# Attention of a hybrid layer: the next pair's sums a unit sooner, a half taken ahead of exponentials, and a first weight's low part put forward

## The reference

```python
def rms_norm(x, g):
    y = xf * lax.rsqrt(jnp.mean(xf * xf, axis=-1, keepdims=True) + RMS_EPS)
    return y * g

x = x + 0.5 * swiglu_ffn(rms_norm(x, ffn1_norm_g), w_gate, w_up, w_down)
proj = rms_norm(x, mix_norm_g) @ w_in
aq = rms_norm(aq.reshape(B, S, 8, 64), attn_q_norm_g)   # 8 heads of 64
ak = rms_norm(ak.reshape(B, S, 8, 64), attn_k_norm_g)
# each chunk of 64 queries sees its own chunk and the 8 before it
scores = einsum('bqhd,bkhd->bhqk', qc, kb) * 64 ** -0.5 + bias
p = softmax(where(key_pos >= 0, scores, -inf))
attn_out = einsum('bhqk,bkhd->bqhd', p, vb)
ro = rms_norm(hgrn2_chunkwise(...), hgrn_out_norm_g) * silu(hg)
x = x + concat([attn_out, ro]) @ w_out
x = x + 0.5 * swiglu_ffn(rms_norm(x, ffn2_norm_g), ...)
```

## Time and profile before

| | us |
|---|---|
| median of 3 runs | 1885.41 (1884.92 to 1886.67) |
| the profiled execution | 1885.16 |
| its span, first to last instruction | 1883.6 |
| TensorE busy | 1869.4 |
| VectorE busy | 1125.0 |
| ScalarE busy | 675.3 |
| GpSimd busy | 406.7 |

### The profile page before, as it was taken

The page is one execution under the profiler, slowest core; times in us unless marked ns, Lnnn a source line. Parts: engine busy times, 40 slices in busy tenths (PEclk is TensorE's granted clock), DMA queues, the critical chain, the costliest instruction groups (busy, mean ns, idle before and its releaser), DMA issues. The chain is left out here.

```text
span 1883.6 us, 24459 instructions
## 1 busy us (share of the span) xinstructions
PE 1869.4 (99%) x9171; PEld 1546.3 (82%) x9171; DVE 1125.0 (60%) x1591; ACT 675.3 (36%) x1029; POOL 406.7 (22%) x319
## 2 busy tenths in 40 slices
PE   9999999999999999999999999999999999999999
PEld 8888888888888888888888678888888888888887
DVE  6966665665546641156667874477666656655464
ACT  7422323333333533211223663353223233333332
POOL 2043422241103110002222310000434222411030
PEclk9999999999999999999999999999999999999999
DMA  5355444436866433434433510133554444368653
GB/s 182 112 196 190 146 162 168 153 138 244 318 195 197 131 122 124 138 101 140 134 132 106 162 60 1 68 112 112 196 190 146 163 167 153 138 244 306 219 192 140
DMA packets 221341, 296.52 MB, mean 157 GB/s; under 512 B 15377, under 2 KB 117913, under 8 KB 221234
## 3 DMA queue, kind: packets, MB, share of 16 engines
q1 hardware_dynamic: 206752, 262.19, 41.0%
q0 software_dynamic: 6272, 18.14, 3.0%
q10 hardware_dynamic: 8210, 14.75, 2.0%
HBM read 206.13 MB, written 92.56 MB: 159 GB/s over the span
## 5 line engine op out<-in xcount | busy, mean ns | idle before, releaser
L710 PE MATMUL ps<-hThi,whi 128*128 128x512 f32 x888 | 346.6, 390 | 0.2 <-DVE hid L1751 0.2
L712 PE MATMUL ps<-hThi,wlo 128*128 128x512 f32 x888 | 345.5, 389 | 0.0
L711 PE MATMUL ps<-hTlo,whi 128*128 128x512 f32 x888 | 345.5, 389 | 0.0
L710 PE MATMUL ps<-whi 128*128 128x512 f32 x616 | 240.0, 390 | 0.0
L712 PE MATMUL ps<-whi,wlo 128*128 128x512 f32 x616 | 239.7, 389 | 0.0
L711 PE MATMUL ps<-wlo,whi 128*128 128x512 f32 x616 | 239.6, 389 | 0.0
L710 PEld LDWEIGHTS ps<-hThi,whi 128*128 128x128 f32 x888 | 166.7, 188 | 34.9 <-issue 0.9
L712 PEld LDWEIGHTS ps<-hThi,wlo 128*128 128x128 f32 x888 | 166.7, 188 | 34.7
L711 PEld LDWEIGHTS ps<-hTlo,whi 128*128 128x128 f32 x888 | 166.7, 188 | 34.3
L710 PE MATMUL ps<-hXhi,whi 128*128 128x512 f32 x480 | 186.9, 389 | 0.8 <-issue 0.8
L712 PE MATMUL ps<-hXhi,wlo 128*128 128x512 f32 x480 | 186.8, 389 | 0.0
(11 more groups left out here) (220 smaller groups left out, 2828.7 us busy)
## 6 DMA issues: line engine op xcount, KB each, us to landing
hid_scratch<-hid SPq DMA_DIRECT2D x132, 256.0 KB, 3.3
raw<-ffn_w_gate SPq DMA_DIRECT2D x44, 512.0 KB, 3.8
raw<-ffn_w_up SPq DMA_DIRECT2D x44, 512.0 KB, 4.9
wdb<-ffn_w_down SPq DMA_DIRECT2D x44, 512.0 KB, 4.1
wd_scratch<-wdb SPq DMA_DIRECT2D x88, 256.0 KB, 4.3
raw<-hid_scratch SPq DMA_DIRECT2D x80, 256.0 KB, 2.8
rawx<-hid_scratch SPq DMA_DIRECT2D x74, 256.0 KB, 2.8
raw<-w_in SPq DMA_DIRECT2D x28, 512.0 KB, 5.4
```

The costliest lines, as they stand in the source:

```text
L710: pe.matmul(dst, ahi, bhi, start=first, stop=False, skip_group_check=onto)
L711: pe.matmul(dst, ahi, blo, start=False, stop=False, skip_group_check=onto)
L712: return pe.matmul(dst, alo, bhi, start=False, stop=last, skip_group_check=onto)
```

## The change

Three things are changed. The squares of the next pair's queries and keys are placed at units 1 and 3 of the pair in place of 1 and 4, their sums at units 2 and 4 in place of 3 and 5; the norms keep their places. ScalarE takes the first turned half ahead of the exponentials of its unit, as it already did with the last; the second and third are still taken behind them. At the start VectorE makes the first weight's low part ahead of the low part of the third tile, and TensorE runs 4 idle products in place of 6 ahead of the first product.

```diff
-SQUARE_AT, SUM_AT, NORM_AT = (1, 4), (3, 5), (6, 8)
+SQUARE_AT, SUM_AT, NORM_AT = (1, 3), (2, 4), (6, 8)
...
-            idle_products(6)
+            idle_products(4)
             products(0, 0, 1)
...
             for v in range(NV + 4):
                 if 2 <= v < NV + 2 and by_scalar(v - 2):
                     take_turned(v - 2)
-                if v < NV - NU and v % NU == TURN_QK_AT[3][2]:
-                    take_half(v // NU + 1, 3)
+                if v < NV - NU:
+                    for n in (0, 3):
+                        if TURN_QK_AT[n][2] == v % NU:
+                            take_half(v // NU + 1, n)
                 if v < NV:
...
                 if v < NV - NU:
-                    for n in range(3):
+                    for n in (1, 2):
                         if TURN_QK_AT[n][2] == v % NU:
                             take_half(v // NU + 1, n)
...
             early_norm(3, 0)
             early_lo_part(1, 0)
+            weight_lo(0, 0)
             early_lo_part(2, 0)
-            weight_lo(0, 0)
             early_lo_part(3, 0)
             weight_lo(0, 1)
```

## The result

The changed kernel takes 1888.97 us (median of 15 executions, 1888.26 to 1890.07), the kernel before 1885.40 (15, 1884.92 to 1886.67). The ratio is 1.0020, 95% interval 1.0012 to 1.0027: slower, and with 3.57 us just inside the 3.8 us (0.2%) within which, by the prediction, this kernel can't be told from no change. The profiled execution took 1888.26 us and its span is 1886.7 us, 3.1 us above the 1883.6 of before. The forecast was 1888.3.

The account below looks back on a forecast made before the run. TensorE, busy 99% of the span, was taken to bound the kernel. Terms: 4.21 us late less 1.15 sooner, net +3.1 on the profiled 1885.16, so 1888.3 us; range 1885.8 to 1890.0.

Parts of the forecast that it names:

- (a): Attention, second and third pair: first sum moved ahead of unit 3's maxima makes the next scores 0.94 us late.
- (b): Attention, second and third pair: second sum moved ahead of unit 5's maxima makes the following scores 0.52 us late.
- S7 to S8: Second pair: time between scores starting at 1061.02 and 1064.94 before the change; forecast 4.86 us in place of 3.92.
- S8 to S9: Second pair: time between scores starting at 1064.94 and 1069.37 before the change; forecast 4.95 us in place of 4.43.
- rival of late squares: Attention: ScalarE's second square ends too late, each pair losing 0.5 to 1 us again, 1889.8 to 1891.3; chance 0.14.
- rival in which the sums cost nothing: Attention: unit 3's maxima don't hold the scores, so only the take and start count, 1884.0 us; chance 0.12.
- only the first sum costs: Rival, attention: second sum and head's output are hidden, 2.98 us late, net +1.8, 1887.0 us; chance 0.10.
- (c): Attention, first pair, without head's output there: two steps between scores become 4.86 (+1.10) and 4.11 us (+0.19), 1.29 late.
- (d): Attention: sooner sums give GpSimd's powers sooner, but the normalising product keeps its place (5.58 us step unchanged), worth nothing.
- (e): Attention, each of three pairs: first turned half taken ahead of unit 7's exponentials, 0.39 us wait goes, 0.35 us gained.
- (f): Kernel start: low part swapped forward and fewer idle products, first product 0.10 us sooner; bounds 0.1 lost to 0.46 won.
- clock rival: Kernel start: granted clock falls, the first product's 12 passes at half clock cost 2.9 us more, 1891.2; chance 0.02.

Follow-up runs that it names:

- the second sum alone: Only the second square and sum moved, to units 3 and 4, against the kernel before: 1890.19 us, ratio 1.0025.
- the moved sums alone: Both squares and sums moved as in the change, start and take left as before, against the kernel before: 1890.25 us against 1885.21, ratio 1.0026.
- the last run: Start and take as changed; second and third pair: squares at units 0, 2, sums 1, 3, norms 5, 7; against the kernel before: 1882.61 us, ratio 0.9986.
- the runs by pair: Squares and sums moved in the first pair only, 1886.76 us, ratio 1.0009; in second and third only, 1888.34, ratio 1.0016; both against the kernel before.

## Why the prediction was right, and where it was not

**(a), (b), the second and third pair: right.** S7 to S8 was forecast at 4.86 us and is 4.87, S8 to S9 at 4.95 and is 4.97. The square ended in time (1067.47 + 1.04 = 1068.51, the sum at 1068.79, 0.28 us to spare where 0.1 was expected), so the rival of late squares didn't happen in the change; the second sum alone shows what it costs when it does. The rival in which the sums cost nothing fell with the moved sums alone. That only the first sum costs fell too: with both moved, 0.5 us stand at S9.

**(c), the first pair: right.** S1 to S2 is 1038.06 - 1033.19 = 4.87 us (4.86), S2 to S3 4.14 (4.11).

**(d): right.** The norm didn't move nearer to S9. In the last run, where the norms move too, S9 to S10 does get shorter.

**(e): right in place, size close.** The wait for the take went, and the maxima took over with 0.16 us, as said. S10 to S11 gained 0.35 us; S11 to the next scores lost 0.04 of it again (4.40 in place of 4.36).

**(f): about the right worth, by luck.** The first product gained 0.35 us, not 0.10. I took the end of ScalarE's high part from one execution, 14.23; in the changed kernel's it began at 13.36 in place of 13.61, and the low part followed at 14.02. That isn't the change's doing: in the profiles of the other runs this high part begins anywhere from 13.04 to 13.74, with the start changed or not. But most of the 0.35 us was given back 14 us later. Five rows of the changed kernel's timeline (PEld is TensorE's weight load, which begins a product; line 1289 keeps the first product's bank):

```profile
14.77 0.50 PE L721 MATMUL ps<-hThi,whi 128*128 128x512 f32 x1
...
27.55 1.03 PE L752 MATMUL ps<-ident,xs 128*128 128x128 f32 x8
...
27.97 0.58 ACT L1289 ACTIVATE gu_s<-ps 128x512 f32<-128x512 f32 x1
...
28.67 0.19 PEld L711 LDWEIGHTS ps<-hThi,whi 128*128 128x128 f32 x1 [0.32 <-issue]
...
31.51 1.03 PE L752 MATMUL ps<-ident,xs 128*128 128x128 f32 x8
```

The same before:

```profile
27.95 1.03 PE L751 MATMUL ps<-ident,xs 128*128 128x128 f32 x8
28.06 0.59 ACT L1288 ACTIVATE gu_s<-ps 128x512 f32<-128x512 f32 x1
...
31.61 1.03 PE L751 MATMUL ps<-ident,xs 128*128 128x128 f32 x8
```

The 0.40 us between the first turns are 0.10 at 31.5. The product between them waits for ScalarE to have kept the first product's bank (`plain_kept`, 27.97 + 0.58 = 28.55), and ScalarE's list had moved by only 0.09 us (28.06 before). ScalarE's list, and not the first product, sets the pace there. Even the 0.10 us isn't shown to come of the change: with only the idle products cut, where the first product kept its 15.12, the same turns stand at 27.92 and 31.53, against the changed kernel's 31.51. The change at the start is worth 0.1 us at most.

**The clock: the failed step.** The prediction read that pauses of 0.8 us hadn't brought the clock down and that the new ones were 1.1 us and less, and put its clock rival at the start, at 0.02. It looked at the pauses' length only, and only at waits for the maxima. The trace of before has one more pause, of TensorE for the first copied turn:

```profile
1036.53 0.74 PE L1044 MATMUL ps<-ident,Pr 128*128 128x128 f32 x5 [1.05 <-DVE PT L2134]
```

It and the new one of 1.04 us stand 0.7 us apart in the changed kernel, and in 6 of 15 executions the mean clock is 0.999, for about 1.2 us. That it falls at this place is read from the profile with all sums moved and from the runs by pair, as the changed kernel's own profile is of the first group. Pauses of 1.41 us standing alone did nothing, so length alone doesn't decide, and that two pauses stand close together fits all runs. By the Trainium skill (TensorE: Matmul & The Clock Gate, "HAM oscillation"), which the prediction held against the idle products, a TensorE that pauses between bursts can fall back to the lower clock; the trace with all sums moved agrees in the first pair of attention, where two pauses of 1.05 and 1.04 us were enough, and no execution with the changed start alone shows a fall.

In sum the spans differ by 3.1 us as forecast, to the tenth only by luck: from the first scores of attention to those that begin the last pair the changed kernel takes 90.56 us (1030.10 to 1120.66) in place of 87.17 (1030.34 to 1117.51), 3.39 us more where parts (a) to (e) give 3.16, and it reached attention 0.24 us sooner, a place that scatters from 1029.69 to 1030.83 between the runs. The executions at clock 1.000 lie 3.25 us above before, and the others lift the median to 3.57.

## What to carry to other kernels

When work of a busy engine is moved within its list, ask which releasing step it now stands ahead of: the sums cost nothing behind the maxima that free the scores and most of their length ahead of them (the first sum 0.94 of its 1.12 us). Sooner inputs gave nothing while the consumer kept its place, and the first round of a loop, where loads are still landing, may need its own places. And a new pause is to be counted together with the old ones beside it: two of a microsecond cost the clock here where one didn't, and work that nothing reads, put into the second, was free.

## What was not expected of the hardware

Four kernels have two pauses of TensorE of 1.05 and 1.04 us with 0.7 us of work between them, and in 6 of 15, 4 of 9, 5 of 11 and 3 of 11 of their executions the mean clock was 0.999; with a pause of 2.84 us it was so in 10 of 11. With the second of the two filled, or without it, it was none of 11, and none of 11 and none of 9, although the last of these has single pauses of 1.41 us. The stretch at half the clock lasted some 3 us and cost 0.9 to 1.9 us of a kernel's time by the two groups of times. Why an execution falls in one group or the other no run shows.
